# Two-phase MLPs of a streaming encoder: sums of the input a tile later, the last set's ReLUs and sums inside the down phase, and the down weights' differences on VectorE instead of GpSimd

## What is computed

```python
def squared_relu_mlp(h, w_up, w_down):
    return jnp.square(jax.nn.relu(h @ w_up)) @ w_down      # 1024 -> 4096 -> 1024
x = x + rms_norm(squared_relu_mlp(rms_norm(x, g2), w_up, w_down), g3)
```

## Time and profile before

| what | value |
|---|---|
| runs | 2453.17, 2456.99, 2457.27 us; median 2456.99 |
| the profiled execution's own time | 2461.53 us |
| its span in the trace | 2459.7 us |
| TensorE busy with matmuls | 2356.7 us (96%) |
| VectorE, ScalarE, GpSimd busy | 1599.3, 1015.4, 966.1 us |
| granted TensorE clock over the span | 0.984 |

### The profile page before, as it was taken

The page is one execution under the profiler, slowest core; times in us unless marked ns, Lnnn a source line. Parts: engine busy times, 40 slices in busy tenths (PEclk is TensorE's granted clock), DMA queues, the critical chain, the costliest instruction groups (busy, mean ns, idle before and its releaser), DMA issues.

```text
span 2459.7 us, 46195 instructions
## 1 busy us (share of the span) xinstructions
PE 2356.7 (96%) x18814; PEld 2215.0 (90%) x18814; DVE 1599.3 (65%) x2469; ACT 1015.4 (41%) x1910; POOL 966.1 (39%) x580
## 2 busy tenths in 40 slices
PE   8999999999899998999999999999999999999997
PEld 7888887799899998999999877689999999999997
DVE  6554454417777778778768344426687778787886
ACT  5554544536433334333326455536533334333321
POOL 0101020115344445677746200114244445677663
PEclk9999999999999999999999999899999999999999
DMA  3101011015243336343325100014323435434334
GB/s 114 44 10 59 19 42 35 30 48 162 94 147 146 146 138 225 134 151 107 133 74 162 60 21 27 26 35 130 123 107 147 146 147 192 163 123 162 115 109 133
DMA packets 117695, 257.42 MB, mean 105 GB/s; under 512 B 11264, under 2 KB 42240, under 8 KB 117536
## 3 DMA queue, kind: packets, MB, share of 16 engines
q1 hardware_dynamic: 109664, 248.62, 29.3%
q10 hardware_dynamic: 7808, 6.56, 0.9%
q0 software_dynamic: 64, 0.10, 0.0%
HBM read 176.79 MB, written 78.45 MB: 104 GB/s over the span
## 4 chain that ended last, share of the span: by engine, by line
PE 68%; DVE 12%; issue 7%; ACT 5%; DMA 4%; POOL 3%; ACTq 0%; SPq 0%; DVEq 0%; POOLq 0%
PE banks L1205 28%; PE banks L298 25%; PE banks L2446 4%; DMA w_raw<-in_units 4%; DVE y L1604 3%; POOL w_raw L240 1%; DVE mlp_s_lo L1513 1%; PE banks L2581 1%; ACT w_hi L253 1%; PE banks L2600 1%; PE banks L1956 1%; PE banks L1937 1%; PE banks L1924 1%; POOL w_raw L243 1%; ACT mlp_s_raw L1389 1%
## 5 line engine op out<-in xcount | busy, mean ns | idle before, releaser
L298 PE MATMUL banks<-h_hi,w_hi 128*128 128x384 f32 (+1 forms) x1416 | 487.8, 344 | 3.7 <-DVE w_lo L269 1.4
L298 PE MATMUL banks<-h_lo,w_hi 128*128 128x384 f32 (+1 forms) x1416 | 467.8, 330 | 0.0
L298 PE MATMUL banks<-h_hi,w_lo 128*128 128x384 f32 (+1 forms) x1416 | 467.2, 330 | 0.0
L230 POOL TENSOR_TENSOR w_lo<-w_raw,w_hi 128x1024 fp32r<-128x1024 f32 x56 | 139.1, 2483 | 800.7 <-ACT w_hi L224 800.7
L261 POOL TENSOR_TENSOR w_lo<-w_raw,w_hi 128x768 fp32r<-128x768 f32 (+1 forms) x164 | 372.4, 2293 | 184.5 <-DVE w_raw L245 147.2
L1604 DVE TENSOR_TENSOR y<-banks,y 128x544 f32<-128x544 f32 x360 | 259.9, 722 | 96.1 <-PE banks L1205 79.5
L1205 PE MATMUL banks<-h_hi,w_hi 128*128 128x272 f32 x1312 | 275.0, 291 | 28.1 <-DVE y L1604 10.2
L298 PEld LDWEIGHTS banks<-h_hi,w_hi 128*128 128x128 f32 x1416 | 268.1, 189 | 27.0 <-issue 18.6
L1205 PE MATMUL banks<-h_lo,w_hi 128*128 128x272 f32 x1312 | 272.2, 289 | 0.0
L1205 PE MATMUL banks<-h_hi,w_lo 128*128 128x272 f32 x1312 | 272.0, 289 | 0.0
L298 PEld LDWEIGHTS banks<-h_lo,w_hi 128*128 128x128 f32 x1416 | 268.3, 189 | 1.9
(11 more groups left out here) (252 smaller groups left out, 5054.4 us busy)
## 6 DMA issues: line engine op xcount, KB each, us to landing
w_raw<-in_units SPq DMA_DIRECT2D x154, 512.0 KB, 3.7
sets_scratch<-mlp_act SPq DMA_DIRECT2D x28, 1088.0 KB, 4.2
h_raw<-sets_scratch SPq DMA_DIRECT2D x56, 544.0 KB, 5.3
sets_scratch<-mlp_act_sums SPq DMA_DIRECT2D x28, 816.0 KB, 5.0
mlp_s_raw<-sets_scratch SPq DMA_DIRECT2D x42, 544.0 KB, 6.4
wide_raw<-in_units SPq DMA_DIRECT2D x26, 512.0 KB, 4.4
x_scratch<-y SPq DMA_DIRECT2D x48, 192.0 KB, 2.4
norm_x<-x_scratch SPq DMA_DIRECT2D x28, 192.0 KB, 3.2
```

The costliest lines, as they stand in the source:

```text
L230: c.nc.gpsimd.tensor_tensor(c.w_lo[:, s], c.w_raw[:, s], c.w_hi[:, s].bitcast(F32), ALU.subtract).then_inc(self.ready, 1)
L298: mm = chip.nc.tensor.matmul(out, w, x, start=(first and n == 0), stop=(last and n == 2))
```

## The change

- `sums_of_h(j)` on VectorE moves behind the take of tile j+1; `gain(j)` on ScalarE moves ahead of its wait for the take of tile j; the two highs of the plain weights move from j = 1, 2 to j = 2, 3.
- The last double leaves out its three ReLUs and puts `mix` of down unit 0 behind product 2. The ReLUs, and then the four sums of the last set, are spread over down units 0 to 6, one behind product 6 of each. The store of the last set moves from unit 0 to unit 8.
- `mix` of down unit d+1 moves from GpSimd to VectorE, behind the take of product 3 of unit d, for all d.
- The lows of the pieces get places behind products 1 and 5 of units p = 1, 2, 3 (two a unit) and, for piece 6, product 1 of p = 0 of the group itself. ScalarE's highs and SyncE's loads of pieces are ordered to match.

```diff
     def high_pair(self, act, unit):
-        ...
+        self.high_blocks(act, unit)
+        self.high_mixed(act, unit)
@@ sync
-                    for i in ((0, 1, 2), (3, 4, 5, 6))[p]:
+                    for i in ((0, 1, 2, 3), (4, 5, 6))[p]:
                         load_piece(g + 1, i)
...
-                    if d == 0:
+                    if d == 2 * PAIRS:
                         store_set(DOUBLES)
@@ scalar
+                if b == NB - 1:
+                    gain(j)
                 act.wait_ge(self.first_taken, self.firsts(n + 1))
...
-                if b == NB - 1:
-                    gain(j)
-                    if j in (1, 2):
-                        ws.high(act, u0 + FIRST_TILES + j - 1)
+                if b == NB - 1 and j > 1:
+                    ws.high(act, u0 + FIRST_TILES + j - 2)
...
+                if p == 0 and g:
+                    high_piece(g, 6)
+                if p and g < GROUPS - 1:
+                    for i in (2 * p - 2, 2 * p - 1):
+                        high_piece(g + 1, i)
...
+                if 0 < d < PAIRS * GROUPS - 1:
                     ws.high_pair(act, self.down_unit(d + 1))
+                elif d == 0:
+                    ws.high_mixed(act, self.down_unit(1))
+                if g == 0:
+                    i, taken = last_squares[p]
+                    act.wait_ge(self.stepped, self.step(DOUBLES - 1, taken))
+                    square(self.act[:, i])
@@ vector
-                if b == NB - 1:
-                    sums_of_h(j)
+                if b == NB - 1 and j:
+                    sums_of_h(j - 1)
+        sums_of_h(FIRST_TILES - 1)
...
+            ws.mix(dve, nc.vector, self.down_unit(0) if last else self.double_unit(n + 1, 0))
             if last:
                 low_piece(0, 0)
-            else:
-                ws.mix(dve, nc.vector, self.double_unit(n + 1, 0))
...
                 take_product(d, i)
+                if d < self.LAST_STEPS and i == 6:
+                    last_set(d)
+                if i == 3 and d < PAIRS * GROUPS - 1:
+                    ws.mix(dve, nc.vector, self.down_unit(d + 1))
...
+                if g and p == 0 and i == 1:
+                    low_piece(g, 6)
                 if g < GROUPS - 1:
-                    piece = {(1, 2): 0, (1, 5): 1, (2, 1): 2, (2, 3): 3, (2, 5): 4, (3, 2): 5, (3, 5): 6}.get((p, i))
-                    if piece is not None:
-                        low_piece(g + 1, piece)
+                    if p and i in (1, 5):
+                        low_piece(g + 1, 2 * (p - 1) + (i == 5))
...
-            if d == 0:
-                sums_of_act(DOUBLES, self.double_squares(DOUBLES - 1, 4))
@@ gpsimd
         for d in range(PAIRS * GROUPS):
-            if d == 0:
-                pool.wait_ge(self.prod_full, self.double_count(DOUBLES - 2, 6))
-            elif d == 1:
-                pool.wait_ge(self.prod_full, self.double_count(DOUBLES - 1, 6))
-            else:
-                pool.wait_ge(self.prod_full, self.down_count(d - 2, 6))
-            ws.mix(pool, ops, self.down_unit(d))
             ws.low_pair(pool, self.down_unit(d))
```

More of the change, by code:

```diff
@@ L245, in mix, with high_blocks @@
         ops.tensor_tensor(of(to, 3), of(to, 2), of(raw, 3), ALU.subtract).then_inc(self.mixed, 1)
-    def high_pair(self, act, unit):
+    def high_blocks(self, act, unit):
         place = self.place(unit)
@@ L251, in high_pair, with high_mixed @@
         self.chip.nc.scalar.copy(hi[:, 0, QUARTER:UNIT], raw[:, 0, QUARTER:UNIT]).then_inc(self.pair_hi, 1)
+    def high_mixed(self, act, unit):
+        hi, _, raw = self.tiles(self.place(unit))
         act.wait_ge(self.mixed, 3 * self.pair(unit) + 3)
         self.chip.nc.scalar.copy(hi[:, 1], raw[:, 1]).then_inc(self.pair_hi, 1)
+    def high_pair(self, act, unit):
+        self.high_blocks(act, unit)
+        self.high_mixed(act, unit)
     def low_pair(self, pool, unit):
@@ L1089, in step @@
     def step(self, n, k):
+        if isinstance(n, int) and n == DOUBLES - 1:
+            k = {self.C21_RAW: self.C12_TAKEN, self.C12_TAKEN: self.C22_TAKEN, self.C22_TAKEN: self.C21_RAW}.get(k, k)
         return self.steps(self.DOUBLE_STEP) + self.STEPS * n + k
@@ L1438, in scalar @@
             nc.scalar.copy(self.halves(self.c22[:]), self.slot_banks(0)).then_inc(self.copied, 1)
[L1439 to L1442, removed]
+            if n == DOUBLES - 1:
+                break
+            ws.high_pair(act, self.double_unit(n + 1, 0))
             act.wait_ge(self.stepped, self.step(n, self.C11_TAKEN))
             square(self.act[:, 0])
-            if last:
-                high_piece(0, 1)
-                high_piece(0, 2)
-            else:
[L1449 to L1461, removed]
+            ws.high_pair(act, self.double_unit(n + 1, 1))
+            for i, taken in ((2, self.C12_TAKEN), (3, self.C22_TAKEN), (1, self.C21_TAKEN)):
+                act.wait_ge(self.stepped, self.step(n, taken))
+                square(self.act[:, i])
+        ws.high_pair(act, self.down_unit(0))
+        for i in range(5):
+            high_piece(0, i)
+        ws.high_blocks(act, self.down_unit(1))
+        for i in range(5, self.N_PROD):
+            high_piece(0, i)
+        last_squares = ((0, self.C11_TAKEN), (2, self.C12_TAKEN), (3, self.C22_TAKEN), (1, self.C21_TAKEN))
         for g in range(GROUPS):
@@ L1583, in double_until_c21, with last_set @@
             combine(n, self.C12_RAW, a12, c22, banks(4), ALU.subtract, self.C22_FULL)
-            relu(n, a12, a12, 0, self.C12_RAW)
-            relu(n, a22, self.c22[:], 1, self.C22_FULL)
             if last:
                 low_piece(0, 3)
+            else:
+                relu(n, a12, a12, 0, self.C12_RAW)
+                relu(n, a22, self.c22[:], 1, self.C22_FULL)
             full(n, 6)
             combine(n, self.C21_RAW, a21, c22, banks(6), ALU.subtract)
-            relu(n, a21, a21, 1, self.C21_RAW)
+            if not last:
+                relu(n, a21, a21, 1, self.C21_RAW)
+        def last_set(n):
+            a11, a21, a12, a22 = (self.act[:, i] for i in range(4))
+            if n == 0:
+                relu(DOUBLES - 1, a12, a12, 0, self.C12_RAW)
+            elif n == 1:
+                relu(DOUBLES - 1, a22, self.c22[:], 1, self.C22_FULL)
+            elif n == 2:
+                relu(DOUBLES - 1, a21, a21, 1, self.C21_RAW)
+            else:
+                sum_of_act(DOUBLES, n - 3)
         def take_product(d, i):
@@ L1635, in vector @@
         take_plain(1)
-        sums_of_act(0, self.squares(PLAIN_TILES))
+        sums_of_act(0)
         for n in range(DOUBLES):
@@ L1639, in vector @@
             if n < DOUBLES - 1:
-                sums_of_act(n + 1, self.double_squares(n, 4))
+                sums_of_act(n + 1)
         for d in range(PAIRS * GROUPS):
@@ L1669, in gpsimd @@
     def gpsimd(self, pool):
-        ws, u0, ops = self.chip.stream, self.unit0, self.chip.nc.gpsimd
+        ws, u0 = self.chip.stream, self.unit0
         self.before.gpsimd(pool)
```

39 lines of the change are left out of this document (21 added, 18 removed).

## The result

The changed kernel takes 2483.76 us (median of 4 runs, 2482.31 to 2487.53), the one before, measured beside it, 2457.13 us (4 runs): ratio 1.0109, 95% interval [1.0085, 1.0132], so 27 us slower. The forecast was slower, 2498 us, within 2462 to 2548. The profiled execution took 2483.5 us with a span of 2481.7. The clock over the span is 0.992, higher than before.

What follows compares the result with a forecast made beforehand. TensorE, busy nearly all the time, was taken as the bound, waiting mainly for VectorE. Start -19, mix +43 and clock +17 made +41 on 2461.5, 2502.5; less 4.5 for the median, 2498 us, range 2462 to 2548.

Steps and rivals of the forecast that it cites:

- part 3: Down units: the mix on VectorE behind take 3 makes GpSimd's lows late, +21.5 us an MLP, +43 for both.
- rival (a): Down-unit crossings: GpSimd keeps the port between its two lows, each crossing costs 0.93 us, 2438 us; chance 0.11.
- (b): Down units: GpSimd's lows are never late, for instance because the mix begins earlier, 2390 us; chance 0.04.
- (d): Down units: VectorE becomes the bound, adding 5 to 10 us, 2505 us; chance 0.06.
- Part 1: Start of each MLP: earlier gains and later sums remove VectorE's idle time, -19 us for both MLPs.
- Part 4, the clock: Down phases: one in four of 40 new 1.9 us waits lowers TensorE's granted clock, +17 us.
- Part 2: Last set's ReLUs, sums and store leave the phase crossing: 6.5 us of copy waits vanish, new places cost nothing.
- VectorE sheds the port waits that made a piece's low cost 2.20 us: Down units: with these port waits shed and longer units, the old waits for takes are all gone.
- 28.2 us is all that the edits there can win: Down phase of each MLP: it takes 322.6 us where its units need 294.4, so 28.2 is the most to win.
- +21.5: Down phase of one MLP: 49.7 us lost to late lows where 28.2 were lost before.

Runs made afterwards that it cites:

- run 2: The changed kernel with the mix on VectorE behind take 0 instead of take 3: 2396.20 us, ratio 0.9745.
- run 11: The kernel before with the new start and the new order and places of the pieces, but the old last set: 2401.96 us, ratio 0.9760.
- run 9: The changed kernel with down units' mixes on GpSimd, the pieces' old places and ScalarE's old order in down units: 2433.65 us, ratio 0.9893.
- run 10: The kernel before with one edit, ScalarE rounding the pieces ahead of the next unit's weights in down units: 2431.70 us, ratio 0.9881.
- run 1: The changed kernel with the down units' mixes back on GpSimd, behind the same waits as before: 2389.81 us, ratio 0.9715.
- run 6: The changed kernel with the mix on VectorE behind take 2 instead of take 3: 2432.38 us, ratio 0.9893.
- run 5: The changed kernel with the mix on VectorE behind take 4 instead of take 3: 2566.79 us, ratio 1.0439.
- run 3: The changed kernel with the second low of a piece (and last-group first-tile lows likewise) behind take 6 instead of 5: 2457.76 us, ratio 1.0000.

## Why the prediction was right, and which of its terms were not

- **The mechanism of part 3 was right, and to the tenth of a us.** The mix was to be done at 8.45 us into a unit, the pair to begin at 8.53 and take 5.28: product 4 starts at 1099.98, so S = 1093.97, and the pair starts 8.53 us later and takes 5.25. The wait was to be 1.89 plus 0.1, and it is 1.76 plus 0.1; where no piece's low comes 0.83 plus 0.1, and it is 0.75 plus 0.1. Down phase: 344 forecast, 342.4 measured. Over both MLPs the down phases grew by 41 us for a forecast of 43. It washed out nowhere, as predicted. So rival (a) fell, GpSimd doesn't keep the ports, and so did (b). But run 2 is what (b) describes, a mix placed earlier: 2396 for its 2390 us. VectorE became no bound either (d), as its 59.6 us of idle time ahead of 136 takes (990 to 1225 us) says.
- **Part 1 was right.** -19 was forecast, -15.5 measured alone, -21 in the spans. The new wait for L230 is 1.43 us for a forecast of 1.8.
- **Part 4, the clock, is the term that failed**: +17 us for one wait in four. In the down phase the clock never fell. The windows over a crossing and behind it (columns as in the earlier trace rows):

```profile
1101.00:1108.00 7.00, 5.40 (x43) 1.00 0.26 75
1107.80:1111.00 3.20, 3.20 (x25) 1.00 0.00 0
```

  The step placed 1.89 us between a wait that had cost the clock and one that had not. The wait that had cost it (2.02 us) was at the start of the doubles, not amid down units. And I had left out the two places where the clock did fall in the down phases of the kernel before, behind waits of 2.29 and 1.20 us (983.89 and 986.99) and behind the second MLP's twin of the 2.98 us wait of the earlier trace rows, 3.03 us at 2092.10:

```profile
987.00:992.20 5.20, 5.20 (x23) 0.50 0.01 3
2092.10:2098.20 6.10, 6.10 (x27) 0.50 0.98 344
```

  So some 2.6 and 3.0 us of the old loss were clock, and the length of one wait is a poor guide in both directions. Why 20 waits of 1.6 us an MLP never cost the clock isn't shown. Without this term the sum is +24, and +27 was measured.
- **Part 2 was put at nothing.** The runs show about -12 us. I had counted its 6.5 us a phase in the earlier trace rows inside the 28.2 us that part 3 replaces, so the sum is not harmed by it. But the low clock behind such a wait (run 11) had no place in my working.
- **The step "VectorE sheds the port waits that made a piece's low cost 2.20 us" has the wrong cause.** I read the earlier trace rows as ports alone and did not follow its idle time, "<-ACT h_hi L1397 3.3", back. It led to ScalarE's queue, where a ready cast stood behind a waiting one. Runs 9 and 10 show it from both sides. The diff had that move in it, and I called it "ordered to match".
- **So "28.2 us is all that the edits there can win" was right, but it was given to the wrong edit.** The other edits alone won all of it: run 1's down phase takes 293.9 us, where 294.4 were said to be needed. The mix on VectorE then cost 48.5 us an MLP and won nothing. My +21.5 stands for the difference of the two. Hence the missed expectation of run 1: I thought the old waits would come back with GpSimd's mix.

## What to carry to other kernels

Place an operation by the chain behind it and not by a free slot on its engine: the mix became half as long on VectorE, but the lows behind it started 4.6 us later in the unit, and they feed TensorE. In a queue that runs in order, put work whose inputs are ready ahead of work that waits; the consumer's idle time ahead of its instruction (here VectorE's, ended by ScalarE) is where such an order shows. And a small net change can hide large terms of both signs, so take it apart before judging it: here -70 and +97 us.

## What the runs showed of the hardware

- Between two GpSimd instructions that follow each other directly, a waiting VectorE instruction with two SBUF operands gets in. It costs GpSimd 1.03 us (5.25 for 4.22 us a pair). VectorE's own low takes 1.28 us when free, 1.72 behind the end of one GpSimd low, and 3.24 to 3.52 when it sits out a whole one (runs 6 and 10). When VectorE's low starts first it keeps its 1.28 us and GpSimd's pair takes 5.27 (run 1). The takes, which read PSUM and one SBUF operand, kept 0.71 to 0.73 us throughout.
- The granted clock stayed at 1.00 over 20 waits of 1.6 us an MLP, one in 12.4 us, and over nearly all pairs of 1.3 and 1.6 us (run 5). It fell behind single waits of 3.9 and 4.1 us (runs 6 and 3). Between these lengths it went both ways: it fell behind 1.79 us in run 5 and stayed at 1.00 behind 1.86 at the same place of the second MLP; in the kernel before it fell behind 2.02 us and behind 3.03, and stayed at 1.00 behind 2.98. Each fall left TensorE at half of the full clock for some 3 to 6 us of its work. The length of the wait alone doesn't tell; what else does was not settled.
